# Second layer's mixer as one stage of rounds over heads, with the chunk-edge differences on GpSimd

## The chip, the cores and the metric

One core of one Trainium2 chip runs the whole program. The metric is the device time of one execution in microseconds (us); of several runs the median is given. Engines are called PE (TensorE), DVE (VectorE), ACT (ScalarE), POOL (GpSimd) and SP (SyncE, which only issues the weight transfers here).

## What is computed

The program computes two small two-layer networks one after the other, for 256 tokens of width 1024. The change touches only one part: the mixer of the second network's second layer (`odd_mixer`), which works on 256 context tokens and 256 latent tokens side by side (512 columns; d is a direction, forward or backward). From the reference, cut:

```python
pl = hl @ w_in                                     # q, gate g, v and two forget maps f (one per direction)
q = silu(pl_q);  v = pl_v
f = lb + (1 - lb) * sigmoid(pl_f);  k = 1 - f;  logf = log(f)
# per head and direction, in chunks of 64 tokens:
gcum = cumsum(logf in the chunk)
k_end = k * exp(g_end - gcum);  chunk_states = k_end^T v
S = exp(g_end) * S + chunk_states                  # carried over 8 chunks, context first
att = causal(q*exp(gcum - g_mid) @ (k*exp(g_mid - gcum))^T)
o = att @ v + (q * exp(gcum)) @ S_in
y = (rmsnorm(o_forward + o_backward) * silu(g)) @ w_out
```

There are 8 heads of 128 channels.

## The kernel before

Tensors lie with channels on the 128 partitions and tokens in the free dimension. Weights stream through `ring`, 12 slots of 128x1024 (512 KB), which SP refills when a slot has been used. A product in three passes (`product_of_parts`, lines 250 to 252) needs each weight tile as a rounded high part and a low rest: ACT casts the tile (L2444, `hg_w_hi`), DVE subtracts (L2483, `hg_w_lo`), and PE multiplies; three such tiles are held (`WB = 3`).

`odd_mixer` is four blocks with barriers between them:

1. `odd_in` projects 40 weight tiles: 8 for q and 8 for g (256 columns each), 8 for v (512 columns, all eight PSUM banks), 16 for the forget maps (512 columns). ACT evacuates each result with Silu, Copy or Sigmoid; DVE then turns the Sigmoid into f (L2507). PE is fed in this order by `w_split`.
2. `log_forget` takes the logarithm of both forget maps on ACT (L2516).
3. `hgrn_scan` loops over heads. Each engine runs through its own program in order and they meet at semaphores. DVE: `decays(h + 1)` makes the running sums (L2567) and the differences that go into the exponentials (L2575 to L2594), for both directions; ACT: `decay_exps` (L2651 to L2654); DVE: `head` multiplies them with k and q (L2600 to L2604); PE transposes k_end (L2680), makes the two attention products (L2686) and the chunk states (L2694); DVE masks the attention (L2621) and runs the carry over chunks (L2633, L2635); PE makes the output from both (L2702, L2707); ACT copies it out (L2664).
4. `hgrn_readout` normalises and projects with `w_out`.

The order is written out by hand; nothing is scheduled by a planner.

Of the kernel before, what the change touches and what calls it, by code (L numbers as in the profile page):

```python
# [7 lines left out]
F32 = mybir.dt.float32  # L8
# [2362 lines left out]
def odd_mixer(k, x, col, gain, shift, gate, hmask, reset):  # L2371
# [7 lines left out]
    with outer:  # L2379
        def sb(name, shape):  # L2380
            return outer.enter_context(nc.sbuf_tensor(name, shape, F32))

        q = sb("hg_q", [P, GH, T])
        sg = sb("hg_g", [P, GH, T])
        v = sb("hg_v", [P, TT, GH * P])
        f = (k.h, k.sq)
        lb = sb("hg_lbs", [P, 3, GH])
        o = q
        lb_in = col("hg_lb")
        with stage_semaphores(nc, "odd_in", *NORM_SEMS, "made", "ready", "rounded", "h_split", "used", "w_rounded", "w_split",  # L2390
                              "kept", "lb1", "lb2") as sems, nc.sbuf_tensor("hg_h_hi", [P, KD, T2], F32R) as h_hi, \
                nc.sbuf_tensor("hg_h_lo", [P, KD, T2], F32R) as h_lo, \
                nc.sbuf_tensor("hg_w_hi", [P, 3, TILES, P], F32R) as w_hi, \
                nc.sbuf_tensor("hg_w_lo", [P, 3, TILES, P], F32R) as w_lo, \
                nc.Block(name="odd_in", no_gpsimd_drain=True) as block:
            norm, (made, ready, rounded, h_split, used, w_rounded, w_split, kept, lb1, lb2) = sems[:4], sems[4:]
            WB = 3
            NS, V0, F0 = 40, 16, 24

            @block.sync  # L2400
            def _(sp):
                k.refill(sp, in_slots, NS, w_split)

            @block.tensor
            def _(pe):
                pe.sem_inc(used, WB)
                norm_tensor(k, pe, norm, T2)
                pe.wait_ge(h_split, KD)

                def tile(n, bank, cols):  # L2410

                    pe.wait_ge(w_split, n + 1)
                    for t in range(KD):
                        mm = product_of_parts(pe, k.ps[:, bank, 0:cols.stop - cols.start], (w_hi[:, n % WB, t, :], w_lo[:, n % WB, t, :]),
                                              (h_hi[:, t, cols], h_lo[:, t, cols]), t == 0, t == KD - 1)
                    mm.then_inc(used, 1)

                for n in range(V0):
                    if n >= 4:
                        pe.wait_ge(kept, n - 3)  # L2420
                    tile(n, n % 4, slice(T, T2))
                pe.wait_ge(kept, V0)
                for t in range(KD):
                    n = V0 + t
                    pe.wait_ge(w_split, n + 1)
                    wh, wl = [w[:, n % WB].rearrange("p (a b) c -> p a (b c)", a=2) for w in (w_hi, w_lo)]
                    for tt in range(TT):
                        tok = slice(tt * P, (tt + 1) * P)
                        for half in range(2):
                            mm = product_of_parts(pe, k.ps[:, tt * 2 + half, :], (h_hi[:, t, tok], h_lo[:, t, tok]),  # L2430
                                                  (wh[:, half, :], wl[:, half, :]), t == 0, t == KD - 1)
                    mm.then_inc(used, 1)
                for m in range(16):

                    pe.wait_ge(kept, V0 + m + 1 if m < 4 else F0 + m - 3)
                    tile(F0 + m, m % 4, slice(0, T2))

            @block.scalar
            def _(act):
                def split(n):  # L2440

                    if n < NS:
                        act.wait_ge(used, n + 1)
# [500 lines left out]
```

## Time and profile before

| | us |
|---|---|
| median of 3 runs (2967.86 to 2973.33) | 2968.55 |
| the profiled execution | 2969.34 |
| its span in the trace | 2967.6 |
| PE busy | 2344.7 (79%) |
| DVE busy | 1757.6 (59%) |
| ACT busy | 1228.8 (41%) |
| POOL busy | 255.2 (9%) |

The profiled execution's own time is its span and 1.7 us around it. The busy shares are means over many stages of which the mixer that is changed is one; its stretches have rows of their own further down.

### The profile page before, as it was taken

How to read it: one execution, taken by the hardware profiler on the slowest of the kernel's cores; microseconds unless marked ns; L12 is line 12 of the kernel's file. 1: busy time of each engine (PE TensorE's matmuls, PEld its weight loads, DVE VectorE, ACT ScalarE, POOL GpSimd, SP SyncE). 2: the span in 40 equal slices, each digit the busy share in tenths (PEclk: the TensorE clock that was granted, in tenths of full speed). 3: DMA queues.
4: the chain of work that ended last, by engine and by line, in shares of the span. 5: the costliest groups of instructions: out<-in, count | busy, mean ns of one | idle time of the engine just before them, and what ended most of it. 6: DMA issues, size and time to landing. Idle time of an engine off the chain costs nothing. (4 is left out here: it accounts for less than half of the span.)

```text
span 2967.6 us, 36574 instructions
## 1 busy us (share of the span) xinstructions
PE 2344.7 (79%) x11964; PEld 1861.0 (63%) x11964; DVE 1757.6 (59%) x2997; ACT 1228.8 (41%) x1849; POOL 255.2 (9%) x329
## 2 busy tenths in 40 slices
PE   4998899899876968766669879996699345579994
PEld 3988666799711856556634467785587344567773
DVE  4763334575201369978850169996422777479994
ACT  2653133464202345441120158884532322158883
POOL 0000000000000257540000001011000000001100
PEclk7999999899999889878879879998799566789997
DMA  4443321344388212110001159997232000269992
GB/s 184 156 161 141 135 72 58 127 160 173 111 341 338 71 50 71 57 36 1 1 0 64 50 215 388 389 389 289 93 113 79 1 0 0 71 257 394 395 397 99
DMA packets 126948, 454.70 MB, mean 153 GB/s; under 512 B 13792, under 2 KB 17504, under 8 KB 126688
## 3 DMA queue, kind: packets, MB, share of 16 engines
q1 hardware_dynamic: 115872, 413.15, 37.0%
q0 software_dynamic: 10944, 39.85, 3.6%
q8 instruction: 76, 1.25, 0.2%
q14 instruction: 56, 0.46, 0.0%
HBM read 431.97 MB, written 20.97 MB: 153 GB/s over the span
## 5 line engine op out<-in xcount | busy, mean ns | idle before, releaser
L2136 DVE TENSOR_TENSOR moe_w_lo<-ring,moe_w_hi 128x1024 fp32r<-128x1024 f32 x384 | 462.9, 1222 | 62.2 <-ACT moe_w_hi L2074 57.2
L2074 ACT CAST moe_w_hi<-ring 128x1024 fp32r<-128x1024 f32 x384 | 399.4, 1050 | 147.4 <-PE ps L252 119.7
L250 PE MATMUL ps<-ffn_h_hi,ffn_w_hi 128*128 128x256 f32 x704 | 205.3, 292 | 33.1 <-DVE ffn_h_lo L369 17.3
L250 PE MATMUL ps<-moe_w_hi,moe_own 128*128 128x512 f32 x512 | 214.1, 418 | 12.2 <-DVE moe_own L2143 11.2
L251 PE MATMUL ps<-moe_w_lo,moe_own 128*128 128x512 f32 x512 | 205.0, 400 | 0.0
L252 PE MATMUL ps<-moe_w_hi,moe_own 128*128 128x512 f32 x512 | 204.8, 400 | 0.0
L251 PE MATMUL ps<-ffn_h_lo,ffn_w_hi 128*128 128x256 f32 x704 | 202.2, 287 | 0.0
L252 PE MATMUL ps<-ffn_h_hi,ffn_w_lo 128*128 128x256 f32 x704 | 202.0, 287 | 0.0
L250 PE MATMUL ps<-even_h_hi,even_w_hi 128*128 128x512 f32 x320 | 139.9, 437 | 75.1 <-DVE even_w_lo L1403 75.0
L359 DVE TENSOR_TENSOR ffn_w_lo<-ring,ffn_w_hi 128x1024 fp32r<-128x1024 f32 x132 | 155.4, 1220 | 69.8 <-ACT ffn_w_hi L326 69.8
L326 ACT CAST ffn_w_hi<-ring 128x1024 fp32r<-128x1024 f32 x132 | 131.4, 1046 | 127.2 <-PE ps L252 70.4
L250 PEld LDWEIGHTS ps<-ffn_h_hi,ffn_w_hi 128*128 128x128 f32 x704 | 138.0, 196 | 40.1 <-issue 39.9
L1392 POOL TENSOR_TENSOR h<-rstd,h 128x241 f32<-128x241 f32 (+14 forms) x120 | 89.5, 767 | 742.3 <-ACT rstd L1332 734.1
L1986 POOL DMA_INDIRECT moe_got<-token_rows,moe_idx x32 | 44.6, 1394 | 1229.7 <-DVE moe_idx L2131 1229.7
L1428 DVE SCALAR_TENSOR_TENSOR h<-sq,cols,h 128x241 f32<-128x241 f32 (+14 forms) x240 | 137.9, 635 | 5.3 <-issue 0.5
L251 PEld LDWEIGHTS ps<-ffn_h_lo,ffn_w_hi 128*128 128x128 f32 x704 | 138.1, 196 | 0.0
L252 PEld LDWEIGHTS ps<-ffn_h_hi,ffn_w_lo 128*128 128x128 f32 x704 | 138.0, 196 | 0.0
L251 PE MATMUL ps<-even_h_lo,even_w_hi 128*128 128x512 f32 x320 | 135.4, 423 | 0.0
L252 PE MATMUL ps<-even_h_hi,even_w_lo 128*128 128x512 f32 x320 | 134.9, 422 | 0.0
L250 PEld LDWEIGHTS ps<-even_h_hi,even_w_hi 128*128 128x128 f32 x320 | 67.0, 209 | 100.4 <-DVE even_w_lo L1403 86.3
L139 PE MATMUL ps<-sq,ones 128*128 128x256 f32 (+1 forms) x224 | 83.6, 536 | 57.7 <-ACT sq L130 56.3
L250 PEld LDWEIGHTS ps<-moe_w_hi,moe_own 128*128 128x128 f32 x512 | 98.2, 192 | 44.9 <-DVE moe_own L2143 14.9
(428 smaller groups left out, 5423.1 us busy)
## 6 DMA issues: line engine op xcount, KB each, us to landing
ring<-in_weights SPq DMA_DIRECT2D x766, 512.0 KB, 5.7
expert_rows<-moe_y POOLq DMA_DIRECT2D x32, 512.0 KB, 7.4
token_rows<-moe_token_rows SPq DMA_DIRECT2D x6, 512.0 KB, 3.4
sq<-in_cmp_w SPq DMA_DIRECT2D x1, 2048.0 KB
both<-in_x SPq DMA_DIRECT2D x1, 1024.0 KB, 5.7
both<-in_context SPq DMA_DIRECT2D x1, 1024.0 KB, 8.0
out<-both SPq DMA_DIRECT2D x1, 1024.0 KB, 4.8
cols<-in_cols SPq DMA_DIRECT2D x1, 724.5 KB, 9.1
```

Source lines behind the costliest of these rows:

```text
L139: mm = pe.matmul(k.ps[:, NORM_BANK, 0:n], k.ones[:, :], k.sq[:, t, 0:n], start=(t == 0), stop=(t == KD - 1))
L250: pe.matmul(out, w_hi, x_hi, start=start, stop=False)
L251: pe.matmul(out, w_hi, x_lo, start=False, stop=False)
L252: return pe.matmul(out, w_lo, x_hi, start=False, stop=stop)
L326: act.copy(w_hi[:, j % WB, half], w).then_inc(w_rounded, 1)
L359: tt = dve.tensor_tensor(w_lo[:, j % WB, half], k.ring[:, (first + 2 * j + half) % RING], w_hi[:, j % WB, half], ALU.subtract)
L1392: pool.tensor_tensor(o, of, o, ALU.add)
L1428: dve.scalar_tensor_tensor(o, i, ftaps[:, m, j:j + 1], o, ALU.mult, ALU.add)
L1986: pool.indirect_dma_start(out=got[:, s, :], out_offset=None, in_=rows_hbm, in_offset=bass.IndirectOffsetOnAxis(ap=idx[:, s:s + 1], axis=0) ...
L2074: act.copy(w_hi[:, j % WB].rearrange("p h f -> p (h f)"), k.slot(act, first + GU + j, e).rearrange("p a f -> p (a f)")).then_inc(w_rounded, 1)
L2136: dve.tensor_tensor(w_lo[:, j % WB].rearrange("p h f -> p (h f)"), k.ring[:, (first + GU + j) % RING].rearrange("p a f -> p (a f)"), w_hi[ ...
```

## The change

`odd_in`, `log_forget` and `hgrn_scan` become one block, `odd`. The v tiles come first and are projected by themselves. Then 11 rounds follow. Round h projects the q tile and the two forget tiles of head h (in rounds 8 and 9 four g tiles each instead), makes the decays, exponentials and weighted operands of head h-1, the attention and states of head h-2, and the output of head h-3. So each engine has, within a round, work on up to four heads. The logarithm is taken on ACT per head and direction with scale and bias (`logs_of`), and k comes from an Identity with scale and bias on ACT. PSUM is divided anew: three banks for projections, one each for transposes, attention and output, two for states.

Of the four differences per direction DVE keeps one (half-chunk, `rin` 1). GpSimd makes the difference to the chunk's edge (`rin` 0) and its two clamps (`rin` 0 at most zero, `rin` 2 at least zero); ACT gets the other signs by a scale of -1. v is read in place, so that its copy (L2563) goes; q's copy of the sums (L2594) goes too. `sg` lies in the context half of x. The weight stream is put in the new order.

```diff
+        sg = x[:, :, 0:T]
...
-        lf_both = sb("hg_lf", [P, 2, GH, T2])
...
-                    act.activation(lf[d], f[d][:, :, :], ACT.Ln)
...
-                            for q_at, k_at, size, ref in ((QM, KM, HC, mid), (QB, KB, GC, edge)):
-                                own = gg[:, T:].rearrange("p (c t) -> p c t", t=size)
-                                refs = own[:, :, ref:ref + 1].broadcast_to([P, T // size, size])
-                                rq, rk = [rel[:, d, i, :].rearrange("p (c t) -> p c t", t=size) for i in (q_at, k_at)]
-                                dve.tensor_tensor(rq, own, refs, ALU.subtract)
-                                dve.tensor_tensor(rk, refs, own, ALU.subtract)
-                            dve.drain()
-                            dve.tensor_scalar(rel[:, d, QB:KB + 1, :], rel[:, d, QB:KB + 1, :], 0.0, None, ALU.min)
-                            dve.tensor_copy(qs[:, s, d, :], gg[:, T:]).then_inc(cum, 1)
...
+            PR, TURN, ATT, STATE, OUT = (0, 1, 2), 3, 4, (5, 6), 7
...
+                def tiles(h):
+                    if h < GH:
+                        return [[F0 + 3 * h + i] for i in range(3)]
+                    at = G0 + 4 * (h - GH)
+                    return [[at, at + 1], [at + 2], [at + 3]] if at < NS else [[], [], []]
+
+                ROUNDS = GH + 3
...
+                @block.gpsimd
+                def _(pool):
+                    for u in range(2 * GH):
+                        d = u % 2
+                        pool.wait_ge(summed_up, u + 1)
+                        if u >= 2:
+                            pool.wait_ge(expd, u - 1)
+                        own, refs = against(gs[d], GC, HC - 1 + d)
+                        pool.tensor_tensor(rin[:, d, 0, :].rearrange("p (c t) -> p c t", t=GC), own, refs, ALU.subtract)
+                        pool.drain()
+                        pool.tensor_scalar(rin[:, d, 2, :], rin[:, d, 0, :], 0.0, None, ALU.max)
+                        pool.tensor_scalar(rin[:, d, 0, :], rin[:, d, 0, :], 0.0, None, ALU.min).then_inc(edged, 1)
...
+                    def project(n):
+                        pe.wait_ge(w_split, n + 1)
+                        if n - F0 < len(PR):
+                            pe.wait_ge(v_kept, n - F0 + 1)
+                        else:
+                            pe.wait_ge(taken, n - F0 - len(PR) + 1)
...
+                        pe.wait_ge(att_kept, 2 * h + 2)
+                        pe.wait_ge(chained, 2 * h + 2)
+                        if h:
+                            pe.wait_ge(kept, h)
...
+                    for h in range(ROUNDS):
+                        places = tiles(h)
+                        if live(h - 3):
+                            mix(h - 3)
+                        if live(h - 2):
+                            turn_ends(h - 2, 0)
+                            attend(h - 2, 0)
+                        for n in places[0]:
+                            project(n)
+                        if live(h - 2):
+                            carry(h - 2, 0)
+                            turn_ends(h - 2, 1)
+                        for n in places[1]:
+                            project(n)
+                        if live(h - 2):
+                            attend(h - 2, 1)
+                            carry(h - 2, 1)
+                        for n in places[2]:
+                            project(n)
...
+                    def exps(h, d):
+                        u = 2 * h + d
+                        act.wait_ge(cum, u + 1)
+                        act.wait_ge(edged, u + 1)
+                        if h:
+                            act.wait_ge(atts, u - 1)
+                        act.activation(ke[:, d, :], ke[:, d, :], ACT.Exp)
+                        act.activation(dec[:, h % 2, d, :], dec[:, h % 2, d, :], ACT.Exp)
+                        act.activation(qs[:, h % 2, d, :], gs[d][:, T:], ACT.Exp)
+                        act.activation(rel[:, d, QB:QM + 1, :], rin[:, d, 0:2, :], ACT.Exp)
+                        act.activation(rel[:, d, KM:KB + 1, :], rin[:, d, 1:3, :], ACT.Exp, scale=-1.0).then_inc(expd, 1)
...
+                    def logs_of(h):
+                        act.drain()
+                        for d in range(2):
+                            if h:
+                                act.wait_ge(cum, 2 * h + d - 1)
+                            act.activation(logs[:, d, :], kx[:, h % 2, d, :], ACT.Ln, scale=lb[:, 1, h:h + 1], bias=lb[:, 0, h:h + 1]
+                                           ).then_inc(logged, 1)
+                        act.drain()
+                        for d in range(2):
+                            act.activation(kx[:, h % 2, d, :], kx[:, h % 2, d, :], ACT.Identity, scale=lb[:, 2, h:h + 1],
+                                           bias=lb[:, 1, h:h + 1]).then_inc(kx_made, 1)
+
+                    for h in range(ROUNDS):
+                        places = tiles(h)
+                        if live(h - 3):
+                            act.wait_ge(mixed, h - 2)
+                            act.activation(o[:, h - 3, :], k.ps[:, OUT, 0:T], ACT.Copy).then_inc(kept, 1)
+                        if live(h - 2):
+                            keep_turned(h - 2, 0)
+                        for n in places[0]:
+                            split(n + WB)
+                        if live(h - 1):
+                            exps(h - 1, 0)
+                        if live(h - 2):
+                            keep_turned(h - 2, 1)
+                        if live(h - 1):
+                            exps(h - 1, 1)
+                        for n in places[0]:
+                            take(n)
+                        for n in places[1]:
+                            split(n + WB)
+                            take(n)
+                        for n in places[2]:
+                            take(n)
+                            split(n + WB)
+                        if live(h):
+                            logs_of(h)
...
+                    def decays(h, d):
+                        u = 2 * h + d
+                        dve.wait_ge(logged, u + 1)
...
+                        dve.sem_inc(summed_up, 1)
+                        own, refs = against(gg, HC, HC // 2 - 1 + d)
+                        dve.tensor_tensor(rin[:, d, 1, :].rearrange("p (c t) -> p c t", t=HC), own, refs, ALU.subtract).then_inc(cum, 1)
+
+                    def weigh(h, d):
+                        u = 2 * h + d
+                        dve.wait_ge(expd, u + 1)
+                        dve.wait_ge(kx_made, u + 1)
...
+                        dve.tensor_tensor(ke[:, d, :], ke[:, d, :], kk, ALU.mult)
+                        dve.tensor_tensor(rel[:, d, QB:QM + 1, :], rel[:, d, QB:QM + 1, :], qh.unsqueeze(1).broadcast_to([P, 2, T]), ALU.mult)
+                        dve.tensor_tensor(rel[:, d, KM:KB + 1, :], rel[:, d, KM:KB + 1, :],
+                                          kk[:, T:].unsqueeze(1).broadcast_to([P, 2, T]), ALU.mult)
+                        dve.tensor_tensor(qs[:, h % 2, d, :], qs[:, h % 2, d, :], qh, ALU.mult).then_inc(rels, 1)
...
+                    for h in range(ROUNDS):
+                        places = tiles(h)
+                        if live(h - 1):
+                            decays(h - 1, 0)
+                        if live(h - 2):
+                            mask(h - 2, 0)
+                        for n in places[0]:
+                            split(n + WB)
+                        if live(h - 2):
+                            chain(h - 2, 0)
+                        if live(h - 1):
+                            decays(h - 1, 1)
+                            weigh(h - 1, 0)
+                        for n in places[1]:
+                            split(n + WB)
+                        if live(h - 2):
+                            mask(h - 2, 1)
+                            chain(h - 2, 1)
+                        if live(h - 1):
+                            weigh(h - 1, 1)
+                        for n in places[2]:
+                            split(n + WB)
...
-    out.append(out_tiles(w[:, :2 * kd]))
+    q_tiles, g_tiles, f_tiles = out_tiles(w[:, :kd]), out_tiles(w[:, kd:2 * kd]), out_tiles(w[:, 3 * kd:])
     out.append(w[:, 2 * kd:3 * kd].reshape(KD, P, kd))
-    out.append(out_tiles(w[:, 3 * kd:]))
+    out.append(np.stack([q_tiles, f_tiles[:GH], f_tiles[GH:]], 1).reshape(-1, P, TILES * P))
+    out.append(g_tiles)
```

ACT before, in the scan: the rows for one head, from its two copies of transposed k_end (`k_end_tok`) to the exponentials of the next head.

```order
L2660 ACTIVATE k_end_tok<-ps 128x512
L2659 REGISTER_ALU
L2660 ACTIVATE k_end_tok<-ps 128x512
L2650 ISA
L2651 ACTIVATE k_end<-k_end 128x512
L2652 ACTIVATE dec<-dec 128x8
L2653 ACTIVATE both<-both 128x256
L2654 ACTIVATE rel<-rel 128x1024
```

ACT after, in a round (h is k_end, kx and transposed k_end; `hg_rin` the differences, `hg_q` the q tile), from the second direction's exponentials to the next round's cast.

```order
L2594 ACTIVATE h<-h 128x512
L2595 ACTIVATE hg_dec<-hg_dec 128x8
L2596 ACTIVATE hg_qs<-rstd 128x256
L2597 ACTIVATE hg_rel<-hg_rin 128x512
L2598 ACTIVATE hg_rel<-hg_rin 128x512
L2608 ACT_TABLE_LOAD
L2608 ACTIVATE hg_q<-ps 128x256
L2562 CAST hg_w_hi<-ring 128x1024
L2612 ACT_TABLE_LOAD
L2612 ACTIVATE h<-ps 128x512 x2
L2562 CAST hg_w_hi<-ring 128x1024
L2619 ACT_TABLE_LOAD
```

The exponentials of one head now stand between evacuations and casts of the projection, and table loads stand between the kinds of function.

DVE before, in the scan, from the second direction's running sum (`g_cum`) to the first carry.

```order
L2579 TENSOR_TENSOR k_end<-g_cum,hg_lf 128x512
L2581 TENSOR_TENSOR g_cum<-dec,k_end 128x512
L2590 TENSOR_TENSOR rel<-g_cum 128x256
L2591 TENSOR_TENSOR rel<-g_cum 128x256
L2590 TENSOR_TENSOR rel<-g_cum 128x256
L2591 TENSOR_TENSOR rel<-g_cum 128x256
L2593 TENSOR_SCALAR rel<-rel 128x512
L2594 COPY both<-g_cum 128x256
L2633 COPY s_in<-ps 128x128
```

DVE after, in a round, from the second direction's running sum (`rstd`) to the second carry.

```order
L2692 SCALAR_TENSOR_TENSOR rstd<-masks,hg_logs 128x512
L2695 COPY hg_dec<-rstd 128x8
L2703 TENSOR_TENSOR h<-rstd,hg_logs 128x512
L2705 TENSOR_TENSOR rstd<-hg_dec,h 128x512
L2709 TENSOR_TENSOR hg_rin<-rstd 128x256
L2717 TENSOR_TENSOR h<-h 128x512
L2718 TENSOR_TENSOR hg_rel<-hg_rel,hg_q 128x512
L2719 TENSOR_TENSOR hg_rel<-hg_rel,h 128x512
L2721 TENSOR_TENSOR hg_qs<-hg_qs,hg_q 128x256
L2657 TENSOR_TENSOR hg_w_lo<-ring,hg_w_hi 128x1024
L2728 COPY_PREDICATED hg_att<-masks,ps 128x256 x2
L2742 COPY hg_s_in<-ps 128x128
```

What moved: three differences, the clamp and the copy are gone from DVE's row, and the weight rest of the projection stands between the weighting of head h-1 and the mask and carry of head h-2.

## Rows read from the trace of the kernel before

**Rows 1.** Busy time by stretch: the mixer's blocks, then one head.

```profile
core 0: us, PE busy (x) PEld busy (x) DVE busy (x) ACT busy (x) POOL busy (x), PEclk, DMA share, GB/s
2114.50:2164.00 49.50, 48.17 (x384) 47.97 (x384) 19.17 (x20) 22.62 (x33) 0.00 (x0) 0.96 0.45 153
2164.00:2208.90 44.90, 43.81 (x192) 35.96 (x192) 9.61 (x8) 8.35 (x9) 0.00 (x0) 1.00 0.30 102
2208.90:2298.80 89.90, 87.34 (x384) 72.00 (x384) 24.84 (x30) 27.28 (x39) 0.00 (x0) 1.00 0.24 82
2298.80:2308.00 9.20, 0.00 (x0) 0.00 (x0) 0.26 (x1) 8.78 (x4) 0.00 (x0) 0.55 0.01 2
2308.00:2514.50 206.50, 101.90 (x608) 90.94 (x608) 165.42 (x418) 45.18 (x89) 0.00 (x0) 0.64 0.00 0
2340.00:2365.20 25.20, 12.54 (x77) 11.29 (x78) 20.52 (x53) 5.57 (x12) 0.00 (x0) 0.64 0.00 1
```

**Rows 2.** Waits in the scan, 2308 to 2515 us.

```profile
PE ps L2702 <- DVE att L2621: 74.5, 7, 10.7
```

**Rows 3.** DVE in order of time in the scan (start, us).

```profile
2486.82 1.22 DVE L2567 TENSOR_TENSOR_SCAN g_cum<-masks,hg_lf 128x512 f32<-128x512 f32 x1
...
2488.43 0.17 DVE L2571 COPY dec<-g_cum 128x8 f32<-128x8 f32 x1
2488.68 0.69 DVE L2579 TENSOR_TENSOR k_end<-g_cum,hg_lf 128x512 f32<-128x512 f32 x1
...
2496.06 0.28 DVE L2633 COPY s_in<-ps 128x128 f32<-128x128 f32 x1
2496.26 0.94 DVE L2621 COPY_PREDICATED att<-masks,ps 128x256 f32<-128x256 int32 x2
2497.30 2.46 DVE L2635 SCALAR_TENSOR_TENSOR s_in<-s_in,dec,ps 128x128 f32<-128x128 f32 x6
```

**Rows 4.** DVE groups by shape, 2114 to 2300 us.

```profile
L2483 DVE TENSOR_TENSOR hg_w_lo<-ring,hg_w_hi 128x1024 fp32r<-128x1024 f32 x37 | 45.3, 1226 | 116.0 <-ACT hg_w_hi L2444 116.0
```

**Rows 5.** PE in order of time at the scan's end.

```profile
2505.43 0.66 PE L2680 MATMUL ps<-ident,k_end 128*128 128x128 f32 x4
2505.92 1.06 PE L2686 MATMUL ps<-rel 128*128 128x128 f32 x8
2506.91 1.16 PE L2694 MATMUL ps<-both,k_end_tok 64*128 64x128 f32 x14
2508.00 0.71 PE L2702 MATMUL ps<-att,both 128*128 128x128 f32 x4
...
2512.92 1.10 PE L2707 MATMUL ps<-both,s_in 128*128 128x64 f32 x8 [1.84 <-DVE s_in L2635]
```

**Rows 6.** ACT in order of time: the first Silu's table load; one direction's exponentials.

```profile
2119.54 1.05 ACT L2444 CAST hg_w_hi<-ring 128x1024 fp32r<-128x1024 f32 x1 [5.81 <-PE ps L252]
2120.61 1.28 ACT L2461 ACT_TABLE_LOAD   x1
2121.90 0.39 ACT L2461 ACTIVATE hg_q<-ps 128x256 f32<-128x256 f32 x1
...
2492.38 0.63 ACT L2651 ACTIVATE k_end<-k_end 128x512 f32<-128x512 f32 x1 [3.46 <-DVE both L2594]
...
2493.32 1.04 ACT L2654 ACTIVATE rel<-rel 128x1024 f32<-128x1024 f32 x1
```

**Rows 7.** POOL's nearest rows by shape, and DVE's weight rests beside them (min/median/max).

```profile
L1392 POOL TENSOR_TENSOR h<-root,h 128x252 f32<-128x252 f32 x8 | 7.2, 896 | 0.7 <-issue 0.7
L1392 POOL TENSOR_TENSOR h<-root,h 128x250 f32<-128x250 f32 x4 | 2.6, 645 | 1.6 <-ACT root L1332 1.1 <-issue 0.5
L1403 DVE TENSOR_TENSOR even_w_lo<-ring,even_w_hi x80: 684/946/1241, 963.5 to 1300.9; 128x512 fp32r<-128x512 f32 x80
```

**Rows 8.** PE after a wait in the first layer's mixer.

```profile
1128.48 0.50 PE L250 MATMUL ps<-even_h_hi,even_w_hi 128*128 128x512 f32 x1 [2.96 <-DVE even_w_lo L1403]
```

**Rows 9.** PE busy, then granted clock, by stretch, around that wait.

```profile
1129.00:1131.00 2.00, 2.00 (x6) 0.50 0.69 233
1131.00:1133.00 2.00, 2.00 (x8) 0.68 0.07 29
```

More of the change, by code:

```diff
@@ new lines, in project @@
+                    def project(n):
[4 more added lines that the diff above has]
+                            pe.wait_ge(taken, n - F0 - len(PR) + 1)
+                        cols = slice(0, T2) if n < G0 and (n - F0) % 3 else slice(T, T2)
+                        for t in range(KD):
+                            mm = product_of_parts(pe, k.ps[:, PR[(n - F0) % 3], 0:cols.stop - cols.start],
+                                                  (w_hi[:, n % WB, t, :], w_lo[:, n % WB, t, :]),
+                                                  (h_hi[:, t, cols], h_lo[:, t, cols]), t == 0, t == KD - 1)
+                        mm.then_inc(used, 1)
@@ new lines, in attend @@
+                    def attend(h, d):
+                        u = 2 * h + d
+                        if u:
+                            pe.wait_ge(att_kept, u)
+                        for j, (q_at, k_at) in enumerate(((QM, KM), (QB, KB))):
+                            for a in range(2):
+                                mm = pe.matmul(k.ps[:, ATT, (2 * j + a) * P:(2 * j + a + 1) * P],
+                                               rel[:, d, k_at, a * P:(a + 1) * P], rel[:, d, q_at, a * P:(a + 1) * P],
+                                               start=True, stop=True)
+                        mm.then_inc(atts, 1)
@@ new lines, in carry @@
+                    def carry(h, d):
+                        u = 2 * h + d
+                        pe.wait_ge(turn_kept, u + 1)
+                        if u:
+                            pe.wait_ge(chained, u)
+                        for c in order(d)[:-1]:
+                            a, r = c // 2, c % 2 * GC
+                            mm = pe.matmul(k.ps[:, STATE[c % 2], a * P:(a + 1) * P], ket[r:r + GC, d, a, :],
+                                           v[r:r + GC, a, h * P:(h + 1) * P], start=True, stop=True)
+                        mm.then_inc(states, 1)
@@ L2751, in _ @@
                     dve.drain()
-                    dve.tensor_tensor(oo[:, a, :], oo[:, a, :], gg[:, a, :], ALU.mult).then_inc(normed, 1)
+                    dve.tensor_tensor(o[:, 2 * a:2 * a + 2, :], o[:, 2 * a:2 * a + 2, :], sg[:, 2 * a:2 * a + 2, :], ALU.mult
+                                      ).then_inc(normed, 1)
                 for m in range(KD):
```

448 lines of the change are left out of this document (184 added, 264 removed).

## The prediction

> **What bounds the kernel now.** The mixer that changes takes, from its first projection matmul at 2114.5 us to the end of its last output at 2514.0 us [rows 1, 5], 399.5 us of the span of 2967.6. I read the stretches first [rows 1]. The reader is to see two halves with different limits. In the projection PE is busy 179 us of 184 at a granted clock of 0.96 to 1.00: it is the bound. For the next 9 us PE has nothing (the logarithms). In the scan, 206 us, no engine is full: in one head of 25.2 us DVE is busy 20.5, PE 12.5, ACT 5.6, and the clock granted to PE is 0.64. The chain of waits says why: PE's output matmuls wait for DVE's masked attention for 74.5 us in total, up to 10.7 at a time [rows 2]. The projection leaves DVE and ACT idle, the scan leaves PE idle. The change puts them side by side, so what counts is no longer one engine's work but the longest circle of waits through a round.
>
> **Engine work per round.** PE: a q tile (48.17 us for 16 tiles at 0.96, so 2.9 each) and two forget tiles (87.34 / 16 = 5.46 each) make 13.8 [rows 1]. Transposes take 0.5 to the next group's start, attention 1.0, states 1.1, twice each; the output is twice 0.71 + 1.10 less overlaps of up to 0.2, so 3.0 [rows 5]. PE has 22.0 us. DVE: at most the 20.5 of a head plus three weight rests of 1.23, 24.2 [rows 1, 4], less what leaves it. ACT: three casts, four table loads of 1.28, exponentials twice 2.0, copies and evacuations: some 19 [rows 6]. So with perfect overlap a round would take about 22 us.
>
> **The circle.** Each engine keeps its written order. I start where DVE ends the second carry of head h-3, since PE opens the round with `mix(h-3)`, which waits for it, and the q tile stands behind that wait. One turn of the circle:
>
> - PE: output 3.0, then transposes 0.5 and attention 1.0 of head h-2, then the q tile 2.9: 7.4.
> - ACT casts the weight tile that may now replace it, 1.05 [rows 6]; DVE makes its rest, 1.15 net of overlap [rows 4]: 2.2.
> - DVE: the first carry of head h-2, 2.65 (0.28 and 2.46 [rows 3]).
> - DVE: the second direction's decays of head h-1: scan 1.22, copy 0.17, two differences of 0.69, four gaps of 0.08 (2488.60 to 2488.68): 3.1 [rows 3].
> - POOL: one difference and two clamps, 128x256. No row shows the clamps. The nearest two-input rows are 0.65 to 0.90 for 250 and 252 columns [rows 7]; I take 0.8 for the difference, 0.55 for a clamp, which reads one input less, and 0.4 for drain and issue: 2.3. Bounds: 0 and 3.1 (three of 0.90 and the drain).
> - ACT: exponentials 2.0 (2492.38 to 2494.36) and 0.1 for the fifth instruction: 2.1. Then a table load and Silu: 1.4 and 0.3, so 1.7 [rows 6].
> - ACT casts the next tile, DVE makes its rest: 2.2.
> - DVE: mask and second carry of head h-2: 2496.06 to 2499.76, net 3.6 [rows 3]. The circle is closed.
> - Six handovers between engines; I allow 0.8 together, chosen.
>
> The sum is 28.0 us. The other three table loads are not in it: the Exp load is done before POOL has finished the first direction, and the Sigmoid and Ln loads come behind the second cast. If that cover went, each would add 1.4. DVE's weighting of the first direction (some 2.3) hides beside POOL and ACT. What leaves DVE (three of four differences, clamp, two copies) would have stood in the decays leg; POOL's 2.3 comes in its place, so that transfer alone buys little.
>
> **The clock.** PE works 22.0 of 28.0 and has most of the rest as one wait of 5 to 6 us before `mix`. The trace has such a wait: after 2.96 us without work [rows 8] the granted clock is 0.50 (the 1.2 GHz level) for two microseconds and 0.68 on average for two more [rows 9], which costs 2 x 0.50 + 2 x 0.32 = 1.64 us of full-speed time. The wait here is longer and the groups behind it are short; I take 1.9. It falls on the circle's PE leg. A steady round is 29.9.
>
> **The whole stage.** Counted from the first v matmul:
>
> - v tiles: 8 x 5.48 [rows 1], cold start 1.9, first copies 1.0: 46.7.
> - Round 0: three tiles 13.8, then Sigmoid, cast, load and Ln 3.9: 17.7.
> - Round 1, no scan on PE yet: ACT's logarithm rest and cast 3.1, rest 1.15, decays 3.1, POOL 2.3, exponentials 2.1, Silu 1.7, cast 1.0, load and two Sigmoids 2.3, cast 1.0, load and Ln 2.2, handovers 0.5: 20.4.
> - Round 2, to the first `mix`: as the circle without its PE leg, with the 3.1 of ACT in place of the cast: 22.8.
> - Five circles, from `mix(0)` to `mix(5)`: 149.5.
> - Round 8 has two g tiles in the first place: 29.9 and 3.1: 33.0.
> - Round 9 has no decays; PE's own order holds it: output 3.0, transposes and attention 1.5, two g tiles 5.8, states 1.1, transposes 0.5, g tile 2.9, attention and states 2.1, carry 2.7: 19.6.
> - The last output: 3.1.
>
> Together 312.8, for 399.5 before: 86.7 less. Norm, readout and the later experts keep their work; the stream is only reordered and a round takes three slots of 512 KB in 30 us, where the projection took one in 3 us [rows 1]. The sum is made against the profiled execution's 2969.3 (0.8 above the median): 2882.6; against the median 2881.9. I round to 2883.
>
> **A page against the row.** In the trace the cast ends at 2120.59, the load starts at 2120.61 and the Silu at 2121.90 [rows 6]: a switch costs 1.4. By the Trainium skill, ScalarE: Activation LUTs, What ACT_TABLE_LOAD costs, a drain of 1.38 us comes on top of each load. By that rule the circle would be 1.3 longer and the time an estimated 2895; by the row it is 2883. The trace disagrees with it, so it gets a small chance.
>
> **The rivals.**
>
> A. The clock stays at 2.4 GHz through the wait. For it: the fall came only at the end of the 2.96 us. Against: the whole scan of before ran at 0.64. Nine rounds without 1.9, less what other legs then take up: 14 us less, 2869.
>
> B. POOL and DVE hinder each other, or the clamps cost more. For it: DVE's rest of 128x512 takes 684 ns at best, 946 in the median and 1241 at worst beside POOL [rows 7]. Three at 0.90 add 0.8 to the circle, 0.3 to 0.5 on each of three or four DVE instructions beside it add up to 1.6, over nine rounds 8 to 22 us: 2891 to 2905.
>
> C. The drain behind each load, above: 2895.
>
> D. PE is the bound after all, if the legs overlap more than the semaphores let me see: 22.0 a round, some 65 us less, 2818. Against: `mix` waits by name for the carry.
>
> E. Slower than before: POOL's leg is a multiple of what its rows say. It decides from 86 / 9 = 9.5 us more per round, a leg of 11.8 instead of 2.3, 3.8 us an instruction. Three of 5 us (13 more a round) would give 3000. Against: no row of that size is near 1 us. This also covers the chance that the rounds overlap nothing and the stage takes what it took.
>
> **How the numbers follow.** The forecast has 0.47 with its own range 2873 to 2892; A 0.20, B 0.20, C 0.05, D 0.03, E 0.03, and 0.02 for no change. The range takes in A and most of B and C: 2862 to 2908. At its low end the bound of POOL at nothing (2.3 x 9 less, but partly taken up elsewhere, about 2867) lies inside too. A change under 0.2%, 6 us, is about what the measurement can't tell from none. All cases but E and no change are faster: 0.95, 0.02 and 0.03.
>
> **What would show it.** In the trace after: rounds of about 30 us from one group of output matmuls to the next; PE waiting once a round, 5 to 6 us, for DVE's carry or mask; a clock near 0.5 for some 4 us behind it; ACT waiting for POOL's clamps before the second direction's exponentials; DVE waiting for the cast after the q tile and again after Silu; three POOL rows per direction with a sum of 2.3; 34 table loads where 5 were. It would be wrong if POOL's instructions were over 1 us, if the wait before the output were under 2 us or over 8, or if the rounds were held by the logarithms instead, that is, if DVE waited for Ln before its scan.

## The result and the profile after

| | before | after |
|---|---|---|
| median (lowest to highest) of 4 runs, us | 2968.2 (2967.45 to 2973.33) | 2897.7 (2892.92 to 2901.16) |
| profiled execution, span, us | 2969.3, 2967.6 | 2892.92, 2890.1 |
| first projection matmul to end of last output (the stage), us | 399.5 | 325.2 |

The ratio is 0.9758 [0.974, 0.9776]: 70.5 us less in the medians. The prediction was 2883 in a range of 2862 to 2908; the median lies inside it, 14.7 above the number. From one execution to the next, the moment at which the stage begins differs by up to 10 us (2110.5 us in the profile of after, up to 2120.3 in those of the experiments), with no edit ahead of it. So I compare the stage's length below, and the medians beside it. A stage length is read from one execution, the profiled one, and that one can lie off its median. The stage was to take 312.8 and takes 325.2.

Busy time of the kernel after by stretch, as in [rows 1]: the v tiles, the rounds to the last output's start, and one round. The columns are those of [rows 1].

```profile
core 0: us, PE busy (x) PEld busy (x) DVE busy (x) ACT busy (x) POOL busy (x), PEclk, DMA share, GB/s
2110.50:2157.00 46.50, 46.50 (x192) 38.06 (x192) 10.92 (x14) 7.33 (x7) 0.00 (x0) 0.93 0.24 79
2157.00:2435.70 278.70, 224.01 (x1377) 201.32 (x1376) 174.10 (x310) 158.83 (x238) 45.18 (x48) 0.87 0.17 57
2284.60:2315.40 30.80, 24.79 (x148) 22.05 (x149) 20.71 (x39) 18.16 (x28) 5.55 (x6) 0.89 0.15 52
```

The two halves lie on each other, as was the idea, but no engine is full in a round: PE is busy 24.79 of 30.80 us, and part of that at half speed. Who waits for whom, in the stage:

```profile
POOL hg_rin L2453 <- DVEq L2707: 225.2, 8, 117.3
DVE hg_w_lo L2657 <- ACT hg_w_hi L2562: 106.9, 28, 6.9
...
ACT h L2594 <- POOL hg_rin L2456: 46.1, 8, 6.6
...
PE ps L2528 <- issue: 32.5, 6, 6.4
```

Behind the colon stand the us waited in total, the number of times and the longest. The first row is an idle helper and costs nothing. In the other three each engine waits for the next one round the circle: DVE for ACT's cast, ACT for POOL's clamps, PE (once a round, 6 us) for DVE's carry, which the view can't name. The same turn in order of time, from one group of output matmuls to the next (start us, us, then engine and line; rows of work off the circle are left out, also where no dots stand):

```profile
2284.61 1.19 PE L2528 MATMUL ps<-hg_att,sq 128*128 128x128 f32 x4 [6.41 <-issue]
2285.60 1.81 PE L2532 MATMUL ps<-hg_qs,hg_s_in 128*128 128x64 f32 x8
...
2290.61 1.15 PE L2505 MATMUL ps<-hg_rel 128*128 128x128 f32 x8
...
2294.67 1.05 ACT L2562 CAST hg_w_hi<-ring 128x1024 fp32r<-128x1024 f32 x1 [3.21 <-PE ps L252]
2295.75 1.23 DVE L2657 TENSOR_TENSOR hg_w_lo<-ring,hg_w_hi 128x1024 fp32r<-128x1024 f32 x1 [2.55 <-ACT hg_w_hi L2562]
...
2299.61 1.22 DVE L2692 TENSOR_TENSOR_SCAN rstd<-masks,hg_logs 128x512 f32<-128x512 f32 x1
...
2302.72 0.91 POOL L2453 TENSOR_TENSOR hg_rin<-rstd 128x256 f32<-128x256 f32 x1 [8.87 <-DVEq L2706]
2303.79 1.10 POOL L2455 TENSOR_SCALAR hg_rin<-hg_rin 128x256 f32<-128x256 f32 x1 [0.16 <-issue]
2304.86 0.85 POOL L2456 TENSOR_SCALAR hg_rin<-hg_rin 128x256 f32<-128x256 f32 x1
2305.79 0.63 ACT L2594 ACTIVATE h<-h 128x512 f32<-128x512 f32 x1 [6.20 <-POOL hg_rin L2456]
...
2307.89 1.28 ACT L2608 ACT_TABLE_LOAD   x1
2309.18 0.38 ACT L2608 ACTIVATE hg_q<-ps 128x256 f32<-128x256 f32 x1
2309.46 1.04 ACT L2562 CAST hg_w_hi<-ring 128x1024 fp32r<-128x1024 f32 x1
2310.53 1.23 DVE L2657 TENSOR_TENSOR hg_w_lo<-ring,hg_w_hi 128x1024 fp32r<-128x1024 f32 x1 [4.40 <-ACT hg_w_hi L2562]
...
2315.43 1.19 PE L2528 MATMUL ps<-hg_att,sq 128*128 128x128 f32 x4 [6.02 <-issue]
```

Read down, each leg starts within about 0.1 us of the end of the one before it. The legs, from the starts and ends of these rows and of those left out between them, beside the prediction's:

| leg | predicted | measured |
|---|---|---|
| PE output, transposes, attention, with the clock's cost | 4.5 + 1.9 | 6.9 |
| q tile | 2.9 | 3.05 |
| cast and rest | 2.2 | 2.2 |
| first carry | 2.65 | 2.7 |
| decays | 3.1 | 3.1 |
| POOL | 2.3 | 3.0 |
| exponentials; load and Silu | 2.1; 1.7 | 2.1; 1.6 |
| cast and rest | 2.2 | 2.2 |
| mask and second carry | 3.6 | 3.7 |
| handovers | 0.8 | 0.3 |
| round | 29.9 | 30.8 |

The five circles from `mix(0)` to `mix(5)` last 31.12, 31.64, 30.82, 31.13 and 32.15 us, so the one read above is the shortest; their mean is 31.4. Clock behind the wait, in stretches of 2 us (PEclk is the last column but two):

```profile
2309.25:2315.43 6.18, 0.16 (x2) 0.03 (x1) 4.38 (x11) 6.07 (x8) 0.00 (x0) 0.94 0.27 85
2315.43:2317.40 1.97, 1.97 (x10) 1.97 (x10) 1.97 (x5) 1.89 (x3) 0.00 (x0) 0.50 0.00 0
2317.40:2319.40 2.00, 2.00 (x11) 2.00 (x10) 2.00 (x3) 0.91 (x2) 0.00 (x0) 0.50 0.00 0
2319.40:2321.40 2.00, 2.00 (x11) 2.00 (x11) 0.51 (x2) 0.39 (x1) 0.00 (x0) 0.50 0.73 254
2321.40:2323.40 2.00, 2.00 (x19) 2.00 (x18) 1.73 (x3) 0.60 (x1) 1.46 (x2) 0.97 0.06 16
```

After 6 us without work PE stands at 0.50, the 1.2 GHz level, for 6 us: the output, transposes and attention, all on the circle. In the rounds of 31.64 and 32.15 us it stays there until 7.1 and 9.1 us behind the output's start, into the q tile; that is why they are longer. After the 2.96 us of [rows 8] the low level lasted 3.4 us (1128.9 to 1132.3), and it began 0.4 us after PE had work again.

### The profile page after: what moved, and what is told of

Read it like the earlier page. It is cut to its first block and busy times, and to the rows that moved or that the text cites. A ratio compares the mean times of both kernels' runs of the same rounds, so it can differ in the third digit from the quotient of the medians.

```text
span 2890.1 us, 36453 instructions
## 1 busy us (share of the span) xinstructions
PE 2331.9 (81%) x11964; PEld 1852.2 (64%) x11964; DVE 1722.6 (60%) x2846; ACT 1281.9 (44%) x1924; POOL 299.8 (10%) x377
## 3 DMA queue, kind: packets, MB, share of 16 engines
q8 instruction: 78, 1.28, 0.2%
## 5 line engine op out<-in xcount | busy, mean ns | idle before, releaser
L130 ACT ACTIVATE sq<-both 128x256 f32<-128x256 f32 (+1 forms) x96 | 35.8, 455 | 215.3 <-PEq L51 211.6
```

Source lines behind the costliest of these rows:

```text
L130: act.activation(k.sq[:, t, 0:n], x[:, t, :], ACT.Square).then_inc(squared, 1)
```

## The experiments

All change the kernel after, except the one that changes the kernel before. "Round" is the mean of the first five pitches of the output groups. "Wait" is the time that PE sits idle ahead of the output in `mix(1)` to `mix(5)`; it shows a change of the circle's other legs without the clock's part.

| kernel | stage us | round us | wait us | median us | ratio to before [95%] |
|---|---|---|---|---|---|
| after | 325.2 | 31.4 | 6.0 to 6.4 | 2897.7 | 0.9758 [0.974, 0.9776] |
| e1, edge back on DVE | 310.5 | 29.3 | 4.3 to 4.6 | 2882.32 | 0.9702 [0.9681, 0.9723] |
| e2, a clamp twice | 337.5 | 33.3 | 7.4 to 7.8 | 2908.61 | 0.9784 [0.9765, 0.9803] |
| e3, q tile before output | 292.2 | 26.8 | 0 to 2.6 | 2868.65 | 0.9652 [0.9631, 0.9672] |
| e4, cast before exponentials | 275.6 | 23.9 | 1.3 to 1.7 | 2848.41 | 0.958 [0.9561, 0.9599] |
| e5, 18 matmuls in the wait | 320.4 | 30.0 | 1.9 to 2.3 | 2884.47 | 0.971 [0.9693, 0.9726] |
| e6, no load for Silu | 312.3 | 29.5 | 4.6 to 5.0 | 2887.08 | 0.9722 [0.9706, 0.9739] |
| e7, no load for Ln | 323.2 | 31.7 | 6.0 to 6.4 | 2890.84 | 0.9732 [0.9716, 0.9748] |
| e8, before with POOL's edge | 398.0 | – | – | 2968.02 | 0.9993 [0.9982, 1.0003] |
| e9, e4 and e1 | 275.4 | 23.5 | 1.5 to 1.9 | 2848.49 | 0.9588 [0.9575, 0.9601] |
| e10, e3 and e4 | 272.2 | 23.7 | 0 | 2845.41 | 0.9579 [0.9566, 0.9592] |
| e11, e10 and an early q take | 267.4 | 23.4 | 0 | 2838.09 | 0.9556 [0.9543, 0.9569] |
| e12, 26 matmuls in the wait | 312.1 | 27.6 | 0 | 2885.11 | 0.9717 [0.9702, 0.9732] |

### What the edge costs on GpSimd (e1, e2, e8, e9)

**e1** takes the GpSimd block out and puts its work into DVE's decays:

```
-    pool.tensor_tensor(... own, refs, ALU.subtract)   # and both clamps
-    act.wait_ge(edged, u + 1)
+    dve.tensor_tensor(rin[:, d, 0, :]..., own, refs, ALU.subtract)
+    dve.drain()
+    dve.tensor_scalar(rin[:, d, 2, :], rin[:, d, 0, :], 0.0, None, ALU.max)
+    dve.tensor_scalar(rin[:, d, 0, :], rin[:, d, 0, :], 0.0, None, ALU.min).then_inc(cum, 1)
```

> The rounds stay, but the difference to the chunk's edge and its two clamps go back to DVE, behind the other difference. The changed kernel's stage takes 325.1 us from the first v matmul to the end of the last output, and a steady round 30.8. Theory (GpSimd's leg of 3.0 us lies on the circle): the decays leg grows by about 1.1 us, 3.1 us of leg and handover go, so a round is 29.0 to 29.3, the stage about 11 to 17 us shorter, the time 2881 to 2887. Rival (DVE is the engine that is short and GpSimd relieves it): DVE's 2.2 us more per round lengthen the round by up to 2.2, the stage by up to 18 us.

The stage is 14.7 us shorter. On DVE the edge's difference (L2694), the drain and the clamps (L2698, L2699), with the other difference (L2696) between them, end 1.3 us after the first starts, by DVE's timeline of e1:

```profile
2299.45 0.43 DVE L2694 TENSOR_TENSOR hg_rin<-rstd 128x256 f32<-128x256 f32 x1
2299.79 0.42 DVE L2696 TENSOR_TENSOR hg_rin<-rstd 128x256 f32<-128x256 f32 x1
2300.28 0.29 DVE L2698 TENSOR_SCALAR hg_rin<-hg_rin 128x256 f32<-128x256 f32 x1
2300.49 0.29 DVE L2699 TENSOR_SCALAR hg_rin<-hg_rin 128x256 f32<-128x256 f32 x1
```

POOL's leg was 3.0, with 0.91, 1.10 and 0.85 for the three. The wait ahead of the output falls by 1.8 us in the mean, about the difference of the legs (3.0 less 1.3). The 14.7 us are not spread evenly: 3.4 come before `mix(0)`, 5.0 in the first circle, where the clock now stays at 1.00 behind the wait, 5.2 in the four circles after it and 1.1 in round 8. The medians are 15.4 us apart. So the part of the change that moves the edge to GpSimd made the kernel slower by about 15 us, and the reordering alone is worth more than the whole.

**e2** doubles one clamp on POOL:

```
+    pool.drain()
+    pool.tensor_scalar(rin[:, d, 2, :], rin[:, d, 0, :], 0.0, None, ALU.max)
```

> One clamp on GpSimd is made twice, with a drain between: 0.85 + 0.16 us more for each direction, and nothing else. Theory (the second direction's edge lies on the circle and the first's does not): a round grows by 1.0, to 31.8, the stage by 8 to 10 us. Rival (hidden behind DVE's weighting): no change. Second rival (both directions on the circle): 2 us a round, 18 in all.

The stage grew by 12.3 us, and a round by 1.9 where I expected 1.0. The added instruction in POOL's order of time:

```profile
2319.75 1.10 POOL L2455 TENSOR_SCALAR hg_rin<-hg_rin 128x256 f32<-128x256 f32 x1 [0.16 <-issue]
2321.00 1.25 POOL L2457 TENSOR_SCALAR hg_rin<-hg_rin 128x256 f32<-128x256 f32 x1 [0.15 <-issue]
2322.22 0.85 POOL L2458 TENSOR_SCALAR hg_rin<-hg_rin 128x256 f32<-128x256 f32 x1
```

The added clamp lasts 1.25 beside DVE, POOL's leg is 4.4, and PE now waits 7.4 to 7.8 us: both grew by 1.4. In three of the five rounds with such a wait the clock is at 0.50 until 9.0 to 9.3 us behind the output's start, and that gives the rest of the 1.9. The second rival, both directions on the circle, had also said 2 us a round. The trace is against it: from the cast behind the q tile to POOL's second direction pass 8.07 us (2310.61 to 2318.68) and in the kernel after 8.05 (2294.67 to 2302.72), so the first direction's added clamp delays nothing there. The place is confirmed; my price per round was half of what it is.

**e8** gives the kernel before (old scan, nothing interleaved) POOL's edge alone:

```
+    pool.tensor_tensor(rq, own, refs, ALU.subtract)
+    pool.tensor_tensor(rk, refs, own, ALU.subtract)
+    pool.drain()
+    pool.tensor_scalar(rel[:, d, QB:KB + 1, :], ..., 0.0, None, ALU.min).then_inc(edged, 1)
-    for q_at, k_at, size, ref in ((QM, KM, HC, mid), (QB, KB, GC, edge)):   # on DVE
+    for q_at, k_at, size, ref in ((QM, KM, HC, mid),):
```

> The kernel before with one part of the change alone: the two differences to the chunk's edge and their clamp (one of 512) go from DVE to GpSimd, in the old scan. There a head is 25.2 us, set by DVE, which gets to the exponentials' results only after its carries of the head before, some 7 us later. Theory (GpSimd pays where its result is wanted late): DVE loses 2 x (2 x 0.34 + 0.5) = 2.3 us a head, the stage 15 to 18 us of 399.5, less 2 to 4 for what DVE's instructions beside GpSimd lose. Rival (GpSimd's leg delays the exponentials and these the head): no gain or slower.

Nothing came of it: 0.9993 [0.9982, 1.0003], though DVE, the scan's bound, has 32 differences and 16 clamps less. I had expected 15 to 18 us less. The rows of POOL and DVE in order of time:

```profile
2359.65 1.04 POOL L2568 TENSOR_TENSOR rel<-g_cum 128x256 f32<-128x256 f32 x1 [15.94 <-DVEq L2600]
2360.13 0.84 DVE L2605 TENSOR_TENSOR rel<-g_cum 128x256 f32<-128x256 f32 x1
2360.66 0.80 POOL L2569 TENSOR_TENSOR rel<-g_cum 128x256 f32<-128x256 f32 x1
2360.90 0.84 DVE L2606 TENSOR_TENSOR rel<-g_cum 128x256 f32<-128x256 f32 x1
2361.61 1.48 POOL L2571 TENSOR_SCALAR rel<-rel 128x512 f32<-128x512 f32 x1 [0.16 <-issue]
2361.66 0.71 DVE L2607 COPY both<-g_cum 128x256 f32<-128x256 f32 x1
2362.29 1.21 DVE L2581 TENSOR_TENSOR_SCAN g_cum<-masks,hg_lf 128x512 f32<-128x512 f32 x1
```

From DVE's first difference to its next scan pass 2.16 us with two differences and a copy; before, 2.05 (2484.77 to 2486.82) with four differences, the clamp and the copy. The differences take 0.84 where they took 0.42, the copy 0.71 where it took 0.29. What DVE saves in instructions it loses in longer ones beside GpSimd, nearly all of it: the second direction, where the first difference still takes 0.43, gains 0.3 us a head.

The Trainium skill, SBUF — State Buffer, two separate sides, has it that a DVE instruction with two SBUF inputs and a GpSimd instruction that reads SBUF exclude each other for their whole length. The trace agrees that they slow each other and not that they exclude: in the kernel after, the last clamp (2304.86 to 2305.71) and DVE's multiplication at L2719 (2304.91 to 2305.81, 0.90) together take 0.95 us, while one after the other the clamp with DVE idle, 0.85 (e2, L2458), and the multiplication's 0.68 without POOL would need 1.5. Spans on POOL are rough, but not by that much.

**e9** joins e1 to e4 (below), to see what the place is worth where the circle no longer runs through POOL:

> The cast ahead of the exponentials (275.6 us for the stage with it alone) and the edge's difference and clamps on DVE. Theory (GpSimd's leg is off the circle now, but while GpSimd works DVE's instructions beside it last up to twice as long, so that it relieves DVE of nothing): within 3 us of the stage with the cast alone. Rival (with the leg covered GpSimd's work is DVE's gain, 2.2 us a round): 10 to 18 us longer. Second rival (GpSimd's leg is still on the circle): 5 to 10 us shorter.

275.4 for e4's 275.6: nothing. On the circle the transfer costs 15 us; off it, in this kernel, it neither costs nor saves.

### Where the circle can be cut (e3, e4, e10, e11)

**e3**, on PE, and **e4**, on ACT, each move one step of a round:

```
 e3 (PE)                                      e4 (ACT)
+    for n in places[0]: project(n)          +    for n in places[1]: split(n + WB)
     mix(h - 3) ... attend(...)                   exps(h - 1, 1)
-    for n in places[0]: project(n)          -        split(n + WB)    # behind the Silu
```

> On PE alone the q tile is projected ahead of the output of head h-3 instead of behind it, so that it no longer waits for the second carry. Theory (the circle runs through output, q tile, cast and rest): q tile, cast and rest (5.2 us) leave the circle and the states (1.1) come in, and the wait ahead of the output gets shorter by the tile: a round of about 27.4, the stage 25 us shorter than 325. Rival (the round is held by ACT's logarithms or by an engine's work): a round stays above 30.

> On ACT alone the cast behind the first forget tile moves ahead of the second direction's exponentials, instead of behind them and behind Silu. DVE's mask and second carry then no longer stand behind a weight rest that waits for GpSimd, exponentials, table load and Silu. Theory: those legs (3.0 + 2.1 + 1.6) leave the circle, DVE's weighting of the first direction (2.4) comes in, and the round falls until PE's 22 us nearly bind: 23.4 to 25, the stage about 275 to 285. Rival (the legs are hidden already and the clock or the handovers make up the round): under 10 us.

e3 takes 33.0 us off the stage (25 expected), e4 49.6. In e3, too, the clock has a part: in four of its first six output groups it stays at the upper level throughout. In e4 the second cast no longer stands behind ACT's wait for POOL. DVE's order puts that cast's rest ahead of the mask and second carry of head h-2, so the cast was the only link by which the decays, POOL and the exponentials of head h-1 delayed them. The waits of e4 in the stage:

```profile
POOL hg_rin L2453 <- DVEq L2708: 194.3, 8, 116.7
...
ACT h L2594 <- POOL hg_rin L2456: 22.5, 8, 5.3
```

ACT still waits for POOL, 22.5 us for 46.1, but nobody waits for ACT there. The output group of e4 in order of time on PE:

```profile
2291.28 0.68 PE L2528 MATMUL ps<-hg_att,sq 128*128 128x128 f32 x4 [1.55 <-issue]
2291.80 1.00 PE L2532 MATMUL ps<-hg_qs,hg_s_in 128*128 128x64 f32 x8
```

PE's wait falls from 6.4 to 1.55 and the output group from 1.19 and 1.81 to 0.68 and 1.00. The shorter wait and the full clock come together, so the gain is larger than the legs that left the circle.

**e10** joins both, **e11** also takes the q tile ahead of the exponentials:

```
+    for n in places[0]: take(n)      # ahead of exps(h - 1, 1)
```

> The cast ahead of the exponentials on ACT and the q tile ahead of the output on PE, edge on GpSimd. Alone they took 49.6 and 33.0 us off the stage of 325.2. Theory (both open the same circle, and PE's 22 us a round are the floor: 8 rounds of 22.0 against 23.8 are all that is left): within 5 us of the cast alone, which has 275.6. Rival (they take different waits away and add up): 260 or less.

> As both orders, and ACT takes the q tile (Silu) ahead of the second direction's exponentials, in its wait for GpSimd, at the price of one more table load a round in the same wait. Theory: the q bank is free earlier and the way to the logarithm is 1.6 us shorter, a round goes from 23.8 towards 22.5 to 23.5, the stage to 266 to 272 us. Rival (the added load of 1.28 us delays the exponentials): the stage longer than with both orders.

e10 adds 3.4 to e4's 49.6: the two cuts open the same circle. e11 is the best version: 0.9556 [0.9543, 0.9569], 2838.09 us, 130 below before and 60 below after. By its timeline PE reaches two output groups in a row straight from a projection matmul:

```profile
2241.95 0.28 PE L252 MATMUL ps<-hg_h_hi,hg_w_lo 128*128 128x256 f32 x1
2242.07 0.61 PE L2528 MATMUL ps<-hg_att,sq 128*128 128x128 f32 x4
...
2265.18 0.28 PE L252 MATMUL ps<-hg_h_hi,hg_w_lo 128*128 128x256 f32 x1
2265.30 0.61 PE L2528 MATMUL ps<-hg_att,sq 128*128 128x128 f32 x4
```

The round shown is 23.2, beside PE's 22.0 of work: here rival D's world begins. A short wait for the states, 1.5 us, remains.

### The clock and the table loads (e5, e12, e6, e7)

**e5** and **e12** fill PE's wait with 18 or 26 matmuls of 512 columns whose product is not used:

```
+    if h > 2: pe.wait_ge(kept, h - 2)
+    for _ in range(26):        # 18 in e5
+        pe.matmul(k.ps[:, OUT, :], h_hi[:, 0, 0:P], h_hi[:, 0, :], start=True, stop=True)
```

> Behind the last projection of a round PE makes 18 matmuls of 512 columns into the output's bank (it waits for its copy first, and the output starts the bank anew), about 4.1 us of the 6.0 that it waits there. Theory (the wait lets the granted clock fall to 0.50, which costs the output, the transposes and part of the attention 2.6 us on the circle): the clock stays at 1.00, a round falls from 31.4 to about 28.8, the stage by 18 to 22 us. Rival (the time behind the wait is something else, such as weight loads of small tiles): no change, or slower where the added matmuls run into the output.

e5 gave 4.8, not 18 to 22. That is read from the slowest of its four executions, 2893.69 us, 9 above their median, and that median is within 1 us of e12's; in the others the stage has probably gained more. Its matmuls last 4.24 us and leave a wait of about 2. The windows of e5 from that wait on (columns as above):

```profile
2251.00:2253.00 2.00, 0.15 (x1) 0.00 (x0) 1.70 (x6) 1.92 (x3) 0.00 (x0) 1.00 0.60 205
2253.00:2255.00 2.00, 1.92 (x14) 1.95 (x15) 2.00 (x4) 1.92 (x3) 0.00 (x0) 0.81 0.00 0
2255.00:2257.00 2.00, 2.00 (x12) 2.00 (x12) 2.00 (x3) 0.95 (x2) 0.00 (x0) 0.50 0.00 0
```

The clock is still at the upper level when the output begins and falls inside it. That is so in three rounds of the first five, 0 to 1.2 us behind the output's start; the other two kept it and lasted 27.8 and 27.9 us for 31.1 to 31.5. POOL's leg is 3.0 in all five, so the clock's price is some 3.5 us a round, and a wait of 2 us can cost as much as one of 6. The first of the two that kept it had no wait ahead of its output, the other had 2.3 us like the rest (and `mix(5)` kept it too, with 1.9); why these kept it, the runs don't tell. In round 9, where PE has no such wait, the added matmuls cost 4.0 us.

> As e5_pe_kept_busy, with 26 matmuls (5.9 us) in place of 18. There 1.9 to 2.3 us without work were left ahead of the output, the clock was still 1.00 when it began and fell to 0.50 within it in three rounds of five. Theory (that rest of the wait is what lets it fall): with 0 to 0.4 us left the clock stays at 1.00 in every round, a round is 27.5 to 28.5, the stage 300 to 306 us. Rival (the small output matmuls themselves let it fall, whatever stands ahead of them): rounds stay at 31.4.

In e12 no wait is left, by PE's timeline:

```profile
2273.14 6.05 PE L2560 MATMUL ps<-hg_h_hi 128*128 128x512 f32 x26
2279.15 0.68 PE L2528 MATMUL ps<-hg_att,sq 128*128 128x128 f32 x4
2279.67 1.00 PE L2532 MATMUL ps<-hg_qs,hg_s_in 128*128 128x64 f32 x8
...
2282.29 1.06 PE L2505 MATMUL ps<-hg_rel 128*128 128x128 f32 x8
2283.11 0.36 PE L250 MATMUL ps<-hg_h_hi,hg_w_hi 128*128 128x256 f32 x1
```

Output, transposes and attention take 3.96 us (2279.15 to 2283.11; 3.9 in the mean of the five) for 6.9, and the rounds 27.6 for 31.4. Not all of these 3.8 us are the clock's, for POOL's leg is 2.45 here instead of 3.0:

```profile
2294.32 0.62 POOL L2453 TENSOR_TENSOR hg_rin<-rstd 128x256 f32<-128x256 f32 x1 [7.54 <-DVEq L2711]
2294.32 0.90 DVE L2714 TENSOR_TENSOR hg_rin<-rstd 128x256 f32<-128x256 f32 x1
```

In the kernel after, with DVE 0.01 us later, it was 0.91 for POOL and 0.43 for DVE; behind it the first clamp takes 0.85 here and took 1.10 there. The same two instructions side by side, and it is once the one engine and once the other that is held up.

The stage misses the expected 300 to 306 because the last two rounds hold the added matmuls too: there PE has no long wait, and the last goes from 19.43 to 25.23 us, nearly their whole 6.05. Work that is thrown away bought 13.1 us of stage; e4 gets more by cutting the circle, after which the wait is short.

**e6** takes q by a plain copy, so the Silu's table load is gone; **e7** takes the logarithm's:

```
 e6:  -  act.activation(..., ACT.Silu)                       +  act.activation(..., ACT.Copy)
 e7:  -  act.activation(..., ACT.Ln, scale=..., bias=...)    +  act.activation(..., ACT.Copy, scale=-1.0)
```

> q is taken by a plain copy instead of Silu, so the output is another; the table load ahead of it goes, the one ahead of Sigmoid stays. Theory (this load is the one of four that lies on the circle): 1.3 to 1.4 us a round, 11 to 13 in the stage, and somewhat more if the wait ahead of the output gets shorter. Rival (a switch also costs a drain behind it): 2.7 a round, 24 in the stage. Second rival (ACT has slack there): nothing.

> The logarithm is replaced by a negated copy, so the output is another; the table load ahead of it goes. Theory (DVE gets to its scan 2.6 us after the logarithm is there, so this load is covered): within 2 us. Rival (the round is held by ACT's work or by the way from the last projection over the logarithm to the scan): 10 us or more.

e6 shortens the stage by 12.9, and the wait ahead of the output by 1.4: one load of 1.28 on the circle, and no drain as long again. Of the 12.9 us 4.7 fall in the first circle alone, where the clock now stays at 1.00, so the stage's length by itself would be a poor measure of the load. e7 gives 2.0 us in the stage and leaves the wait as it was, 6.0 to 6.4: the load behind the second cast is covered, as the prediction had it. (Its profiled execution is its slowest; its median is 6.9 us below that of the kernel after, and which part of the program this comes from is open.)

## Why the prediction was right, and where its sum was short

**The circle** was right, leg by leg and in its order. It is shown by the table above, by e2 (a POOL leg 1.4 us longer makes PE's wait 1.4 longer), e6 (an ACT leg 1.3 shorter makes it 1.4 shorter), e7 (a load off it leaves it as it was), and e4 (cut, the rounds fall to 23.9).

**Where the 12.4 us of the stage are.** Up to `mix(0)` 111.4 for 107.6 predicted, the five circles 156.9 for 149.5, round 8 34.7 for 33.0, round 9 19.4 for 19.6, the last output 2.9 for 3.1: 3.8 + 7.4 + 1.7 - 0.2 - 0.2. Two terms of the circle were mis-sized. They are the 7.4 us of the five circles and act in round 8 too; of the 3.8 before `mix(0)`, where PE has no long wait yet, POOL's leg in rounds 1 and 2 makes some 1.5, and the rest is open:

- *POOL 2.3.* It measured 3.0. I had priced a clamp at 0.55 because it reads one input less. A clamp takes 0.85 with DVE idle (e2), and the two-input difference 0.62 at its shortest (e12): one input less saves GpSimd nothing. At these lengths the leg is 2.45, as in e12, since the difference is cheaper than my 0.8. The other 0.55 is DVE working beside it, which makes the difference 0.91 and the first clamp 1.10. The upper bound, 3.1, would have been the better choice.
- *The clock 1.9.* It measured some 3.5 a round (e5). The PE leg was to be 4.5 at full clock and 6.4 with its cost; it is 3.9 at full clock (e12) and 6.9 in the round read, 7.1 in the mean of the five circles, and the q tile loses some tenths too. I had read 1.64 from a wait of 3 us [rows 9] and added a guess, where small matmuls after 6 us of waiting stay at 0.50 for 6 to 9 us.

So the clock was 1.6 short and POOL 0.7, and a round is only 1.5 longer than forecast, because two other terms were too large: the PE leg at full clock by 0.6 and the handovers, 0.3 for 0.8 in the round read, by 0.5. That these offset nearly half of the two misses is luck; without them the median would have come out near the upper end of the range. One sign that I had named for being wrong, a POOL instruction over 1 us, did appear (1.10 for the first clamp, 1.05 for the first direction's difference), and it pointed at the right term.

**The rest up to the median.** The profiled execution is 76.4 below before's, which is the stage's 74.3 and 2.1 elsewhere; the medians are 70.5 apart. That last difference lies in single executions.

**The rivals.** *A* (the clock stays) fell: it is at 0.50 behind each wait, and where e5 and e12 hold it up the round is 3.5 to 3.8 shorter. *B* (POOL and DVE hinder each other, clamps dearer) is half true. The clamps are dearer and on the circle. The hindering is large on DVE (the multiplication at L2717 takes 1.11 beside POOL, 0.69 without), but in a round DVE has time there, so that side costs nothing. On POOL's side it lies on the circle and costs 0.55 us a round. In e8, where DVE is the bound, it eats nearly the whole gain. *C* (a drain behind each load, from the Trainium skill's ScalarE: Activation LUTs, What ACT_TABLE_LOAD costs) fell with e6: doubling the load's cost would have given some 24 us and a wait 2.7 shorter, and 12.9 and 1.4 came. *D* comes up only in e10 and e11, where PE no longer waits ahead of the output. *E* (slower) needed a POOL leg of 11.8.

**What I passed over.** "That transfer alone buys little" was too kind: by my own legs it put 2.3 in the place of the 0.9 or so that DVE needs, and e1 shows that it costs 15 us. The change made the kernel faster by its reordering alone.

## What to carry to other kernels

When engines keep a written order and pass work round, find the closed circle of waits and add up its legs: here it came within 1.5 us of a round, where PE's 22.0 us of work would have been 9 off, and it shows which single step to move. Here moving one cast ahead of one wait was worth 50 us, as much as two thirds of the whole change. A wait on TensorE just before small matmuls was paid twice here, since the clock fell with it; and since it fell in some rounds and not in others, read a leg's change from the wait as well as from the stage. Work moved from VectorE to GpSimd cost 15 us on the circle and bought next to nothing off it or in the old scan; I would want it off every circle and beside an idle VectorE, a case that no run here has.

## What was unexpected in the hardware

- A one-input clamp on GpSimd, 128x256 in fp32, takes 0.85 us with DVE idle (e2) and up to 1.41 beside DVE; DVE alone takes 0.29. The two-input difference of the same size took 0.62 in e12, less than the clamp.
- Beside GpSimd, DVE's two-input instructions of 256 columns went from 0.42 to 0.84 us and a copy from 0.29 to 0.71, yet the two overlapped more than strict turns would allow.
- After 4 us of dense matmuls and 2 us without work the clock was still at the upper level when a group of small matmuls began, fell 0 to 1.2 us into it and stayed low for some 7 us, in three rounds of e5; after the same in two others it did not fall. What tells them apart stays open.
